# Modulation products moved into the ring of transposed-P banks, value products one step later, output sums ahead of maxima, and small transfers reissued in another order

## The reference, cut to what matters

```python
sh_a, sc_a, ga_a, sh_f, sc_f, ga_f = split(silu_c @ w_mod + b_mod, 6)     # and the same for the context
h = modulate(rms_norm(x, g_attn), sh_a, sc_a)
q, k, v = split_mixer_inputs(h @ w_in, qk_g)        # per-head RMS norm of q and k; rotary in groups A and C
p = softmax(q k^T / 8 + mask or bias, and a sink logit in A); o = p v     # A: window, B: neighbourhood + bias, C: global
x = x + ga_a * (o @ w_out)
x = x + ga_f * swiglu(modulate(rms_norm(x, g_ffn), sh_f, sc_f), w_gate, w_up, w_down)
```

## Time and profile before

| | |
|---|---|
| median of three runs | 1993.47 us (1987.88 to 1995.14) |
| profiled execution | 1989.94 us, span 1988.1 us |
| busy share of the span | PE 88%, weight loads 74%, DVE 46%, ACT 24%, POOL 44% |
| DMA | 174.40 MB, mean 88 GB/s |

### The profile page before, as it was taken

The page is one execution under the profiler, slowest core; times in us unless marked ns, Lnnn a source line. Parts: engine busy times, 40 slices in busy tenths (PEclk is TensorE's granted clock), DMA queues, the critical chain, the costliest instruction groups (busy, mean ns, idle before and its releaser), DMA issues.

```text
span 1988.1 us, 29853 instructions
## 1 busy us (share of the span) xinstructions
PE 1755.9 (88%) x11057; PEld 1473.8 (74%) x11057; DVE 915.5 (46%) x1621; ACT 478.6 (24%) x945; POOL 872.0 (44%) x671
## 2 busy tenths in 40 slices
PE   5899937887796999999999997996686979999998
PEld 2588826776685888888888885885575758888887
DVE  3545436676516554154514536355697342223132
ACT  2212325565403010001000113224575132001010
POOL 0244318656142444445444452540400546666664
PEclk9999868899798999999999997998898989999999
DMA  8144333323021432243323321443200223333332
GB/s 286 43 110 118 85 74 101 96 69 103 22 64 53 127 112 89 65 125 116 106 63 114 102 79 42 110 110 81 59 2 1 64 64 95 95 94 92 91 90 97
DMA packets 316391, 174.40 MB, mean 88 GB/s; under 512 B 87550, under 2 KB 307598, under 8 KB 316302
## 3 DMA queue, kind: packets, MB, share of 16 engines
q1 hardware_dynamic: 288608, 148.54, 26.7%
q10 hardware_dynamic: 27694, 24.66, 3.9%
HBM read 159.04 MB, written 2.83 MB: 81 GB/s over the span
## 4 chain that ended last, share of the span: by engine, by line
PE 75%; DVE 12%; issue 3%; SPq 3%; POOL 2%; DMA 2%; ACT 2%; ACTq 0%; DVEq 0%; POOLq 0%
PE acc L679 62%; DVE stat L1464 3%; DVE prob_t L1478 2%; PE acc L650 2%; SPq L445 2%; PE mod_ps L750 1%; PE small L860 1%; POOL split_w L526 1%; DVE o_sum L1490 1%; PE acc L827 1%; PE acc L828 1%; SPq L414 1%; PE small L925 1%; PE side L845 1%; DVE inv L1261 1%
## 5 line engine op out<-in xcount | busy, mean ns | idle before, releaser
L679 PE MATMUL acc<-act,split_w 128*128 128x512 f32 x5088 | 1009.1, 358 | 38.1 <-DVE act L1305 32.5
L679 PEld LDWEIGHTS acc<-act,split_w 128*128 128x128 f32 x5088 | 836.6, 190 | 190.8 <-issue 34.5
L526 POOL TENSOR_TENSOR split_w<-raw_w,split_w 128x1024 fp32r<-128x1024 f32 (+1 forms) x220 | 528.8, 2403 | 18.4
L523 POOL TENSOR_SCALAR split_w<-raw_w 128x1024 fp32r<-128x1024 f32 (+1 forms) x220 | 228.2, 1037 | 389.0 <-PE acc L679 203.4
L679 PE MATMUL acc<-hidden,split_w 128*128 128x512 f32 (+1 forms) x1584 | 309.6, 357 | 0.1
L679 PEld LDWEIGHTS acc<-hidden,split_w 128*128 128x128 f32 x1584 | 261.8, 188 | 46.5 <-DVE hidden L1551 0.6
L522 POOL TENSOR_TENSOR turnstile<-ones 128x1 f32<-128x1 f32 x136 | 54.7, 402 | 464.8 <-PE acc L679 464.8
L1325 DVE SCALAR_TENSOR_TENSOR x_t<-acc,mod,x_t 128x512 f32 (+1 forms) x96 | 60.5, 658 | 303.3 <-PE acc L679 303.3
L1549 DVE TENSOR_TENSOR prod<-acc,silu_g 128x768 f32<-128x768 f32 (+1 forms) x44 | 36.3, 824 | 332.7 <-PE acc L679 332.7
L860 PE MATMUL small<-v,prob_t 128*128 128x128 f16 x696 | 87.4, 229 | 102.4 <-DVE o_sum L1490 92.1
L860 PEld LDWEIGHTS small<-v,prob_t 128*128 128x128 f16 x696 | 66.1, 103 | 120.5 <-issue 100.5
(11 more groups left out here) (150 smaller groups left out, 1564.0 us busy)
## 6 DMA issues: line engine op xcount, KB each, us to landing
raw_w<-in_w_gate SPq DMA_DIRECT2D x44, 512.0 KB, 3.8
raw_w<-in_w_up SPq DMA_DIRECT2D x44, 512.0 KB, 3.8
mod_chunk<-in_w_mod ACTq DMA_DIRECT2D x22, 1024.0 KB, 5.0
raw_w<-in_w_mod SPq DMA_DIRECT2D x36, 512.0 KB, 3.8
raw_w<-in_w_in SPq DMA_DIRECT2D x64, 256.0 KB, 3.7
raw_w<-in_w_down SPq DMA_DIRECT2D x32, 512.0 KB, 4.1
mod_start<-in_w_mod SPq DMA_DIRECT2D x4, 2048.0 KB, 13.7
ks<-q_split SPq DMA_DIRECT2D x64, 96.0 KB, 2.1
```

The source lines that it names most:

```text
L523: pool.tensor_scalar(split_w[slot][:, 0, 0:n, :], raw_w[slot][:, 0:n, :], 1.0, 0.0, ALU.mult, ALU.add).then_inc(hi_w, 1)
L526: pool.tensor_tensor(split_w[slot][:, 1, 0:n, :], raw_w[slot][:, 0:n, :], split_w[slot][:, 0, 0:n, :].bitcast(F32), ALU.subtract).then_inc ...
L679: mm = pe.matmul(acc[slot][:, a:b], split_w[slot][:, part == 2, k, :], moving[:, part == 1, k, a:b], start=(k == 0 and part == 0), stop=(k ...
```

## The change

1. **Modulations in the ring.** Each modulation unit takes one of the three banks of `turned_at`, as if it were a chunk of a transposed P. `bank_order` writes down the order of chunks and modulations, and `free_bank` waits for what last used the bank. The new steps (`mod_steps`) follow the number of keys processed, about one modulation per 1280 keys from step 2 on; PE does a modulation at the end of its step, behind the value products, instead of ahead of the scores. ACT (`take_modulation`) now takes the turned values of the unit before out with the bias vector added (an Identity activation of 128x2), besides the row copy; DVE's two adds at the end go. POOL's splits follow the new steps.
2. **Value products at g-4** instead of g-3, with a fourth buffer `prob_t`.
3. **Output sums first.** DVE sums the outputs of a group at the head of the step 4k+8, ahead of `top_of`; before, at step 4k+7, behind `minus_top`.
4. **Late input work** on DVE and ACT moves by a step or so (`norm_tile` at steps 2, 6, 7; `round_low` at 1, 4, 8, 9; `round_high` at 3, 7, 8).
5. **SP's order.** The rows of inverse norms and the stacks of units 12 and 13 go ahead of the bias rows; in layer 0 the loads of modulations 2 and 3 as well, half of the bias rows follow, then the stacks of units 14 and 15, and the other half is spread between the next eight modulation loads. In layer 1 the first two loads of `w_out` (12 DMAs) go ahead of the row of unit 13. POOL makes the bias tables after groups 8 to 11.

```diff
-MOD_STEP = {2 + 2 * (n * 5 // 4): n for n in range(len(ATTN_MOD))}
+def mod_steps():
+    out, keys, n = {}, 0, 0
+    for i, g in enumerate(LAYER_STEPS[0]):
+        keys += STEPS[g]["n"]
+        if n <= len(ATTN_MOD) and i >= 2 and keys >= 1000 + 1280 * n:
+            out[i] = n
+            n += 1
+    return out
...
+def bank_order():
+    out = []
+    for l in range(DEPTH):
+        for i in range(len(LAYER_STEPS[l]) + 4):
+            if 2 <= i < len(LAYER_STEPS[l]) + 2:
+                g = LAYER_STEPS[l][i - 2]
+                out += [("p", upto(g, n_chunks) + c) for c in range(len(STEPS[g]["chunks"]))]
+            if l == 0 and i in MOD_STEP:
+                out.append(("m", MOD_STEP[i]))
+    return out
...
# SP
+                stack_up(l, 8)
                 inv_to_dram(l, 12)
-                stack_up(l, 8)
+                stack_up(l, 9)
                 inv_from_dram(l, 12)
-                stack_up(l, 9)
...
+                else:
+                    load_out(0)
+                    load_out(1)
                 inv_to_dram(l, 13)
                 inv_from_dram(l, 13)
...
+                inv_to_dram(l, 14)
+                inv_from_dram(l, 14)
+                inv_to_dram(l, 15)
+                stack_up(l, 12)
+                inv_from_dram(l, 15)
+                stack_up(l, 13)
                 if l == 0:
                     load_mod(2)
                     load_mod(3)
...
+                for h in range(2):
+                    for r in range(ROWS):
+                        load_bias(h, r)
                 stack_up(l, 14)
                 stack_up(l, 15)
                 if l == 0:
                     for n in range(4, len(ATTN_MOD)):
                         load_mod(n)
+                        if n < 12:
+                            for r in range(2):
+                                load_bias(2 + (n - 4) // 4, 2 * ((n - 4) % 4) + r)
...
# PE
+            def free_bank(item):
+                before = BANK_AT[item] - 3
+                if before < 0:
+                    return
+                kind, c = BANKS[before]
+                if kind == "p":
+                    pe.wait_ge(prob_lo, c + 1)
+                elif c < len(ATTN_MOD):
+                    pe.wait_ge(mod_row_ready, c + 1)
+                else:
+                    pe.wait_ge(mod_taken, c)
...
-                for g in range(g0, g1 + 3):
-                    if l == 0 and g - g0 in MOD_STEP:
-                        pe.wait_ge(exps, g - 1)
-                        modulation(MOD_STEP[g - g0])
+                for g in range(g0, g1 + 4):
...
-                    if g0 <= g - 3 < g1:
-                        weigh(g - 3)
+                    if g0 <= g - 4 < g1:
+                        weigh(g - 4)
+                    if l == 0 and g - g0 in MOD_STEP:
+                        modulation(MOD_STEP[g - g0])
...
# ACT
+                def take_modulation(n):
+                    ps = turned_at[BANK_AT["m", n] % 3]
+                    if n < len(ATTN_MOD):
+                        sc.wait_ge(unit_done, u_mod(n) + 1)
+                    if n:
+                        ll, m = ATTN_MOD[n - 1]
+                        sc.wait_ge(mod_turned, n)
+                        sc.activation(mod[:, ll, m, :], ps[:, P:P + 2], ACT.Identity, bias=vecs[:, 64 * ll + m:64 * ll + m + 1]
+                                      ).then_inc(mod_taken, 1)
+                    if n < len(ATTN_MOD):
+                        sc.activation(mod_row[n % 2][:, :], ps[0:4, 0:P], ACT.Copy).then_inc(mod_row_ready, 1)
...
# DVE
-                for g in range(g0, g1 + 4):
+                for g in range(g0, g1 + 5):
+                    if (g - g0) % 4 == 0 and g - g0 >= 8:
+                        sum_outputs((g - g0 - 8) // 4)
                     if g < g1:
                         top_of(g)
                         minus_top(g)
-                    if (g - g0 - 4) % 4 == 3 and g - g0 >= 7:
-                        sum_outputs((g - g0 - 4) // 4)
```

More of the change, by code:

```diff
@@ L154, in is_biased @@
     return s["bias"]
+def mod_steps():
[6 more added lines that the diff above has]
+    return out
+MOD_STEP = mod_steps()
+MOD_AT = {n: i for i, n in MOD_STEP.items()}
+assert len(MOD_AT) == len(ATTN_MOD) + 1
 def is_new_sink(s):
@@ L221, in trunk @@
         prob = [place(f"prob{i}", [P, TOK + 4], F32, a0 + i * 3136) for i in range(3)]
-        prob_t = [place(f"prob_t{i}", [P, 2, TOK], F16, a0 + 9408 + i * 3072) for i in range(3)]
+        prob_t = [place(f"prob_t{i}", [P, 2, TOK], F16, a0 + (9408, 12480, 15552, 41664)[i]) for i in range(4)]
         bias = [place(f"bias{i}", [P, 3, 256], F32, a0 + 18624 + i * 3072) for i in range(4)]
@@ L417, in _, with load_out @@
             for l in range(DEPTH):
+                def load_out(j):
+                    u = u_out(l) + j
+                    sp.wait_ge(split_ready, u - 1)
+                    for half in range(2):
+                        rows = raw_w[u % 2][64 * half:64 * half + 64]
+                        for k0, n, r0, step in ((0, 3, 192 * half, 64), (3, 2, 384 + 64 * half, 128), (5, 3, 640 + 192 * half, 64)):
+                            src = bass.AP(w_out.tensor, (l * D + r0) * D + P * j, [[D, 64], [step * D, n], [1, P]])
+                            sp.dma_start(rows[:, k0:k0 + n, :], src).then_inc(raw_in[u % 2], 16)
                 for j, (_, _, _, cols) in enumerate(QKV):
@@ L461, in _ @@
                         load_mod(n)
-                def load_out(u, col):
-                    for half in range(2):
-                        rows = raw_w[u % 2][64 * half:64 * half + 64]
-                        for k0, n, r0, step in ((0, 3, 192 * half, 64), (3, 2, 384 + 64 * half, 128), (5, 3, 640 + 192 * half, 64)):
-                            src = bass.AP(w_out.tensor, (l * D + r0) * D + col, [[D, 64], [step * D, n], [1, P]])
-                            sp.dma_start(rows[:, k0:k0 + n, :], src).then_inc(raw_in[u % 2], 16)
-                for j in range(4):
-                    u = u_out(l) + j
-                    sp.wait_ge(split_ready, u - 1)
-                    load_out(u, P * j)
-                for j in range(4, KT):
-                    u = u_out(l) + j
-                    sp.wait_ge(split_ready, u - 1)
-                    load_out(u, P * j)
+                        if n < 12:
+                            for r in range(2):
+                                load_bias(2 + (n - 4) // 4, 2 * ((n - 4) % 4) + r)
+                else:
+                    for h in range(2, 4):
+                        for r in range(ROWS):
+                            load_bias(h, r)
+                for j in range(0 if l == 0 else 2, KT):
+                    load_out(j)
                 for ch, n in enumerate(CHUNKS):
@@ L1155, in _ @@
                     if l == 0 and g - g0 in MOD_STEP:
-                        n = MOD_STEP[g - g0]
-                        sc.wait_ge(unit_done, u_mod(n) + 1)
-                        if n >= 2:
-                            sc.wait_ge(mod_turned, n - 1)
-                        sc.activation(mod_row[n % 2][:, :], acc[0][0:4, 896:1024], ACT.Copy).then_inc(mod_row_ready, 1)
-                    if g - g0 in (2, 6, 7):
-                        round_high({2: 13, 6: 14, 7: 15}[g - g0])
+                        take_modulation(MOD_STEP[g - g0])
+                    if g - g0 in (3, 7, 8):
+                        round_high({3: 13, 7: 14, 8: 15}[g - g0])
                 w = width(l)
```

94 lines of the change are left out of this document (38 added, 56 removed).

## The result

The changed kernel takes 1900.88 us, the median of four runs (1899.58 to 1903.83), where the kernel before, run four times beside it, takes 1990.68 (1987.83 to 1995.14): a ratio of 0.955 [0.952, 0.958]. The forecast said 1918. The profiled execution took 1899.58 us, its span 1897.8: 90.3 us less than before, against 73.7 in the sum.

A forecast was written before the change was run, and what follows sets the result against it. Dense products (62% of the chain) stay; attention is bound by SP-order stalls, elsewhere DVE's pace. Layer 0 47.3 plus layer 1 28.4 less 2 gives 73.7 us: 1918. Own range 1897 (everything at floors) to 1945; 8-in-10 range 1896 to 1952.

The forecast's parts named there:

- Start of layer 0: Steps 0 to 11: SP's new order brings modulation 2's load earlier; exponential 12 at 291 instead of 310.3, saving 19.3 us.
- The second wait: Layer 0, step 10: modulation 4's load stands behind 16 bias rows and the stacks of units 14 and 15; some 8 us.
- context steps: Layer 0's 256-key stretches, steps 24 to 35 and 60 to 79, charged at full addition: 8.2 and 9.6 us saved.
- C: Layer 0, steps 36 to 59: between PE's floor 61.7 and full addition 70.9, 65 taken instead of 69.9; 4.9 us saved.
- Steps 12 to 23: Layer 0, group A, six modulations: between PE's floor 8.0 and full addition 10.1 per group, 9.5 taken; 4.4 us saved.
- Group B of layer 0: Steps 80 to 95: 34.9 us from layer 1, less three times 0.58, plus 0.85 per modulation, gives 37.4; 0.9 us saved.
- bubbles: DVE idle of 0.58 us per group of four ahead of the next maximum, removed by summing `small` first.
- Layer 1: Waits of 7.2 and 13.5 us go, with five 0.58 us idle gaps in A and ten in C and B: 28.4 us.
- the cover for PE's wait: Value products two iterations behind DVE's low part hide PE's earlier wait for the sum; if not, 0.58 us per group stays.
- Smaller edits: 36 Identity activations on ACT, ACT's queue waits, bank waits and the tail: 2 us lost, as ACT has slack.
- the slower rival: Identity not in the exponential's table set: each `take_modulation` switches twice, 92 us more, 2010 us; chance 3%.
- Lockstep: Rival: ring and ACT's wait couple PE, ACT and DVE; each of 36 modulations costs 1.3 us more, 1965 us; chance 11%.

The follow-up runs named there:

- one-product runs: Changed kernel with one of each modulation's 16 products: 1888.43 us; the same with layer 0's bias tables after groups 15 to 18: 1879.49 us (single runs).
- late sums: Changed kernel with the output sums behind the maximum of their step again, still step 4k+8: 1952.96 us, 0.980 of the kernel before.
- order: Changed kernel with SP's old order of transfers in both layers, all else as changed: 1934.10 us, 0.971 of the kernel before.
- place: Changed kernel with each modulation ahead of the scores of its step, still in the ring: 1933.46 us, 0.970 of the kernel before.
- delay: Changed kernel with value products at g-3 again and output sums at the head of step 4k+7: 1906.23 us, 0.957 of the kernel before.
- second round: Changed kernel with loads of modulations 2 to 5 issued earlier, among rows and stacks, and bias rows spread later: 1880.28 us, 0.944 of the kernel before.
- the filler: Kernel of the late sums plus 12 unread products on TensorE ahead of each wait for the sum: 1931.89 us, 0.971 of the kernel before.

## Why the prediction was right, and where its sizes were off

- **Start of layer 0** (19.3 forecast): right, step by step. PE's product of modulation 2 came at 260.8 (262.6 forecast), that of modulation 4 at 283.7 (284.7), exponential 12 at 290.6 (291). The saving is 18.7 us, and the experiments with SP's order give it nearly all to that order: undone, 15.0 us come back, and put into the kernel before it saves 16.8. The second wait was foreseen but taken as given; earlier loads remove both waits, another 18.7 us of this stretch.
- **Steps 12 to 59 and the context steps.** C 5.9 us saved (4.9 forecast), context 7.9 and 10.7 (8.2 and 9.6): right. Steps 12 to 23 6.5 (4.4): the 26.4 us lie midway between the floor (24.0) and the 28.5 chosen, and PE is busy for 25.7 of them, so PE and not DVE's pace sets the length there. The forecast named PE's floor and POOL's load in C; that they are two near-equal bounds needed the pair of one-product runs. PE's waits for splits in C, 3.3 us in the forecast, are 0.9 in the trace.
- **Group B of layer 0** is the mis-sized term: 0.9 forecast, 7.4 measured. I charged each of five modulations 0.85 us, the price that before showed for one ahead of the scores. At the end of the step it costs nothing where DVE sets the pace: with modulations B takes 30.9 us, in layer 1 without them 31.3. Put ahead of the scores again they cost 3.5 there, 0.7 each. The rest of the error is in the base, 34.9: it came from a layer-1 stretch at a granted clock of 0.90 (last window of before above), and loses 3.6 with its bubbles, at a clock of 1.00, not the 1.7 of 3 x 0.58.
- **Layer 1** (28.4): 29.0. A 21.5 of 22.6, C and B 7.5 of 5.8. DVE's wait for unit 13's row is 0.9 us, so the 0 taken was right. C runs at 52.7/6 = 8.8 per group, as forecast; DVE goes from the sum to the next maximum without idle time, kernel after:

```profile
1388.95 1.01 DVE L1529 TENSOR_TENSOR prob_t<-side,prob_t 128x512 f16<-128x512 f32 x2
1389.88 0.17 DVE L1537 RECIPROCAL stat<-stat 128x4 f32<-128x4 f32 x1
1389.96 0.66 DVE L1541 TENSOR_REDUCE o_sum<-small 128x256 f32<-128x512 f32 x1
1390.54 0.95 DVE L1515 TENSOR_REDUCE stat<-acc 128x1 f32<-128x768 f32 x1
```

- **What hides the sum.** I gave the later value products as the cover for PE's wait. That reason fell: at g-3 layer 1 keeps its gain but for 0.6 us. What counts is that the sum stands ahead of the maximum: PE's six waits for it in C of layer 1 fall from 10.5 to 3.9 us. I also priced the bubble as DVE's idle time alone, and so did the expectation of the late sums; its other part, TensorE's clock, was not in the sum at all.
- **Smaller edits** (2 us lost): not to be seen. The Identity activations take 0.26 us each (the 14 that are not shown the same), and ahead of the exponentials there are two table loads, one per layer; source views after:

```profile
L1192 ACT ACTIVATE mod<-side,vecs x22: 251/262/280, 244.7 to 452.8; 128x2 f32<-128x2 f32 x22
...
L1181 ACT ACT_TABLE_LOAD  x2: 1283/1283/1283, 235.5 to 1302.5; - x2
```

So the slower rival was void. The Trainium skill, "ScalarE: Activation LUTs", section "Table sets: the hidden batching unit", had said so; now the rows agree with it: 36 Identity activations run among the exponentials with no load at them.

The sum in all: layer 0 57.2 for 47.3, layer 1 29.0 for 28.4, 4.1 outside both, and the 2 not lost: 90.3 - 73.7 = 16.6. The 1900.9 measured lie at the fast end of the range, but not for the reason given for that end, layer 0's A and C at their floors: they are 2.4 and 2.3 us above. What led there is B, the 2 us and the 4.1 outside the stages, so the range held there by its width, which is luck. Its end is also mis-added: 3.3, 4.5, 8 and 2 us below 1918 is 1900, not 1897. (Steps 24 to 35 held five modulations before, not six; no sum uses that.)

*Lockstep* was wrong, yet it names what the modulation ahead of the scores does, 33 us.

The parts don't add up: order 33, sums 52, place 33 and delay 5 make 123, not 90. Each was undone in a kernel in which little else waited, so that a new wait makes others late; for the sums it also costs clock. In the place's 33 us there is little of it: from step 12 to the end of the context steps the granted clock stays at 1.00 there. That the parts overlap in this way is argued, not shown; only SP's order was tried from both sides.

## What to carry to other kernels

On a queue that issues in order, write down for each transfer when it is first needed and when its own wait ends, and sort by that: it was worth 33 us here and 21 more in a second round. Put optional work of the bounding engines behind everything that others wait for, and the step that frees a shared buffer ahead of a long one. When two engines are each about full in a stretch, taking work from one shows little: take it from both to see the next bound.

## What was not expected of the hardware

Waits of TensorE of about 2 us, once in four steps, can be followed by stretches at the lower clock. With the late sums (waits of 1.7 us) layer 1's group A had a granted clock of 0.83 and took 59.8 us; with the same waits partly filled by products nobody reads 0.97 and 53.8; with the sums first 0.94 and 53.1. In group C the filler brings 1.00 for 0.94, and 56.4 for 59.7 us. So beside the 31 us that the waits cost at most, the clock behind them cost 21 at least, although DVE is what sets the pace there.

The wait alone does not decide it. Of six equal waits in group C of the late sums two were followed by half speed, and of the six in the kernel before none: there C took 56.6 us at 1.00, as long as the filled kernel's. What else decides is not shown by these runs.
